# Summing the experts' outputs in DRAM with accumulating indirect transfers instead of one-hot matmuls, and a fourth weight slot while the experts run

## What is computed

```
aff = softmax(xt @ w_router)
gate, idx = top_k(aff.T, cap)                      # cap = 2 * n / 16
xe = take(xt, idx)
hid = silu(xe @ w_gate) * (xe @ w_up)
ye = (hid @ w_down) * gate[..., None]
y = zeros_like(xt).at[idx.reshape(-1)].add(ye.reshape(-1, D))
x = x + gt2 * y
```

## Time and profile before

| | |
|---|---|
| median of 3 runs | 3823.74 us (3815.38 to 3830.78) |
| the profiled execution's own time | 3816.27 us |
| its span | 3814.5 us |
| TensorE busy | 3627.5 us, 95% |
| VectorE busy | 1238.6 us, 32% |
| ScalarE busy | 832.8 us, 22% |
| GpSimd busy | 92.1 us, 2% |
| mean TensorE clock granted | 0.979 |
| moved by the DMA engines | 655.29 MB, mean 172 GB/s |

### The profile page before, as it was taken

How to read it: one execution, slowest core, us unless ns; L and a number is a source line. 1 busy time by engine, 2 the same in 40 slices (tenths; PEclk the granted TensorE clock), 3 DMA queues, 4 the chain that set the end, 5 groups by cost and what they waited for, 6 DMA issues and landing times.

```text
span 3814.5 us, 49841 instructions
## 1 busy us (share of the span) xinstructions
PE 3627.5 (95%) x21913; PEld 2043.0 (54%) x21913; DVE 1238.6 (32%) x2319; ACT 832.8 (22%) x1791; POOL 92.1 (2%) x112
## 2 busy tenths in 40 slices
PE   6999999998999799999999999999999988999997
PEld 3557777775555334343455577677655543443433
DVE  1444333337441400000142644333463531000102
ACT  2122112225332211100121311221343330110101
POOL 1000000000100000010000000000000000000000
PEclk9999999999999899999999999999999998999999
DMA  7332342323242599989742332341522327999892
GB/s 203 94 74 83 84 115 59 94 45 124 88 163 76 189 375 379 369 304 329 279 127 67 101 91 69 87 103 37 160 68 95 130 75 282 386 377 349 301 338 102
DMA packets 213272, 655.29 MB, mean 172 GB/s; under 512 B 8970, under 2 KB 21496, under 8 KB 209344
## 3 DMA queue, kind: packets, MB, share of 16 engines
q1 hardware_dynamic: 199680, 615.54, 47.5%
q0 software_dynamic: 7568, 23.32, 2.4%
q10 hardware_dynamic: 5808, 13.24, 0.9%
HBM read 600.45 MB, written 51.61 MB: 171 GB/s over the span
## 4 chain that ended last, share of the span: by engine, by line
PE 89%; DMA 5%; DVE 3%; ACT 2%; issue 1%; ACTq 0%; POOL 0%; DVEq 0%; SPq 0%; POOLq 0%
PE unit L735 11%; PE unit L683 10%; PE unit L1206 10%; PE work L1209 8%; PE work L1206 6%; PE unit L747 3%; PE unit L726 3%; PE work L1160 3%; PE unit L1105 3%; PE unit L766 3%; DMA ring<-in_w_e_gate 3%; PE unit L677 3%; PE unit L1054 2%; PE work L931 1%; PE work L936 1%; PE unit L693 1%
## 5 line engine op out<-in xcount | busy, mean ns | idle before, releaser
L735 PE MATMUL unit<-hT,ring 128*128 128x512 f32 x1024 | 478.5, 593 | 0.0
L1206 PE MATMUL unit<-ring,arena 128*64 128x512 f32 x2048 | 464.0, 600 | 2.6 <-ACT arena L1647 2.1
L1209 PE MATMUL work<-ring,arena 128*32 128x256 f32 x6144 | 367.2, 382 | 6.0 <-DMA ring<-in_w_e_gate 5.8
L1206 PEld LDWEIGHTS unit<-ring,arena 128*64 128x64 f32 x2048 | 141.1, 138 | 289.9 <-issue 283.9
L1209 PEld LDWEIGHTS work<-ring,arena 128*32 128x32 f32 x6144 | 182.0, 109 | 207.4 <-issue 93.2
L735 PEld LDWEIGHTS unit<-hT,ring 128*128 128x128 f32 x1024 | 176.5, 191 | 131.9 <-issue 131.9
L1206 PE MATMUL work<-ring,arena 128*64 128x512 f32 x1024 | 234.2, 599 | 4.0 <-ACT arena L1661 2.1
L683 PE MATMUL unit<-hT,ring 128*128 128x512 f32 x512 | 221.1, 592 | 0.0
L683 PE MATMUL unit<-arena,ring 128*128 128x512 f32 x384 | 166.8, 592 | 0.0
L683 PEld LDWEIGHTS unit<-hT,ring 128*128 128x128 f32 x512 | 96.7, 190 | 118.6 <-issue 118.6
L2101 DVE COPY arena<-work 64x512 f32<-64x512 f32 x32 | 22.2, 694 | 421.9 <-PE work L1206 421.9
(11 more groups left out here) (405 smaller groups left out, 4856.4 us busy)
## 6 DMA issues: line engine op xcount, KB each, us to landing
ring<-in_w_e_gate SPq DMA_DIRECT2D x64, 2048.0 KB, 11.5
ring<-in_w_e_up SPq DMA_DIRECT2D x64, 2048.0 KB, 9.6
ring<-in_w_e_down SPq DMA_DIRECT2D x64, 2048.0 KB, 10.7
ring<-in_w_in SPq DMA_DIRECT2D x32, 2048.0 KB, 15.0
ring<-in_w_ada SPq DMA_DIRECT2D x24, 2048.0 KB, 9.2
spill<-xT SPq DMA_DIRECT2D x110, 256.0 KB, 9.9
arena<-spill SPq DMA_DIRECT2D x20, 1280.0 KB, 7.3
ring<-in_w_out SPq DMA_DIRECT2D x4, 2048.0 KB, 7.9
```

The lines of the kernel that those rows point to most:

```text
L735: last = mm(bank[:, :], w[:, k, m * P:(m + 1) * P], hT[:, k, 0:TS], start=k == 0, stop=k == KD - 1)
L1206: last = mm(big[SLS * c:SLS * c + SLS, :], x, w[:, kk, 512 * c:512 * c + 512], start=k == 0, stop=k == KD - 1)
L1209: last = mm(low[SLOTP * c:SLOTP * c + SLOTP, 0:256], xp, w[:, kk, 256 * c:256 * c + 256], start=k == 0, stop=k == KD - 1)
```

## The change

The one-hot products are gone, and with them `ST`, `STP`, `iota`, the side work and the last pass. A tensor `moe_sum` of 640 rows in DRAM takes their place in each layer:

- During the attentions POOL clears it with five copies of 512 KB from a block of zeros in the constants, DRAM to DRAM.
- The copies of an expert's results multiply by the gate and write all 80 rows to one of three tiles `Y`.
- POOL adds these 80 rows to the rows of `moe_sum` with one indirect accumulating transfer, two experts behind the gathers in its order, each one only after the one before has landed.
- After the last of them ACT reads `moe_sum` back (five transfers of 512 KB into `ysum`), TensorE turns it, and DVE adds it to `xT` as before.

Beside this, the space of `h2tok` is a fourth slot for weights while the experts run (`slot_of`, `slot_before`): its first chunk waits for the stores of `h2_rows`, and chunk c then waits for chunk c - 4.

The diff, cut to its core:

```diff
-SIDE_SLOTS = [(_e, _w) for _e in range(1, NE + 1) for _w in "dm"]
-PASSES = [range(0, 4), range(4, 6), range(6, 8)]
...
+MRING = RING + 1
+assert PRE_CHUNKS % RING == 0 and NMOE % MRING == 0
+
+
+def slot_of(c):
+
+    l, q = c // LAYER_CHUNKS, c % LAYER_CHUNKS
+    if q < PRE_CHUNKS:
+        return q % RING, l * (PRE_CHUNKS // RING + NMOE // MRING) + q // RING + 1
+    s, n = (q - PRE_CHUNKS) % MRING, (q - PRE_CHUNKS) // MRING + 1
+    if s == RING:
+        return s, l * (NMOE // MRING) + n
+    return s, (l + 1) * (PRE_CHUNKS // RING) + l * (NMOE // MRING) + n
+
+
+def slot_before(c):
+
+    l, q = c // LAYER_CHUNKS, c % LAYER_CHUNKS
+    if q < RING:
+        return c - MRING
+    if q < PRE_CHUNKS + MRING:
+        return c - RING
+    return c - MRING
 
 
...
+        ring.append(at(15872, (4096,)))
...
-        YP = [at(13824, (D,))] + [at(8192 + D * g, (D,)) for g in range(NPT - 1)]
-        Ysc = [at(14848, (D,))] + [at(D * j, (D,)) for j in range(NPAIR - 1)]
-        ST = hT[:, 0:7, :].rearrange("p k t -> p (k t)")[:, 0:NPAIR * TS].rearrange("p (j t) -> p j t", j=NPAIR)
-        STP = hT[:, 7, 0:NPT * TP].rearrange("p (j t) -> p j t", j=NPT)
+        Y = [at(D * i, (D,)) for i in range(NROWS)]
+        ysum = at(15872, (NT, D))
...
-                    name, value = chunk_used(c - RING)
+                if c == PRE_CHUNKS + RING or c == LAYER_CHUNKS + PRE_CHUNKS + RING:
+                    sp.wait_ge(sig["rows_moved"], 16 * NT * (2 * (c // LAYER_CHUNKS) + 1))
+                elif c >= RING:
+                    name, value = chunk_used(slot_before(c))
                     sp.wait_ge(sig[name], value)
...
+                for t in range(NT):
+                    pool.dma_start(moesum[l][tile_t(t), :], A["consts"][:, CSTW:CSTW + D]).then_inc(sig["scattered"], 16)
...
-                for e in range(NE):
-                    if e >= NROWS:
-                        pool.wait_ge(sig["rows_turned"], l * NE + e - NROWS + 1)
-                    pool.indirect_dma_start(picked[e % NROWS][0:SL, :], None, h2rows[l],
-                                            bass.IndirectOffsetOnAxis(token[:, e:e + 1], 0))\
-                        .then_inc(sig[f"rows{e % NROWS}_loaded"], 16)
+                for e in range(NE + 2):
+                    if e < NE:
+                        if e >= NROWS:
+                            pool.wait_ge(sig["rows_turned"], l * NE + e - NROWS + 1)
+                        pool.indirect_dma_start(picked[e % NROWS][0:SL, :], None, h2rows[l],
+                                                bass.IndirectOffsetOnAxis(token[:, e:e + 1], 0))\
+                            .then_inc(sig[f"rows{e % NROWS}_loaded"], 16)
+                    if e >= 2:
+                        s = e - 2
+                        pool.wait_ge(sig["left_copied"], l * NE + s + 1)
+                        pool.wait_ge(sig["right_copied"], l * NE + s + 1)
+                        pool.wait_ge(sig["scattered"], 16 * (l * (NT + NE) + NT + s))
+                        pool.indirect_dma_start(moesum[l], bass.IndirectOffsetOnAxis(token[:, s:s + 1], 0),
+                                                Y[s % NROWS][0:SL, :], None, compute_op=ALU.add)\
+                            .then_inc(sig["scattered"], 16)
 
 
...
                         expert_chunk(e - 1, "d0")
-                        side_work((e, "d"))
                         expert_chunk(e - 1, "d1")
-                        side_work((e, "m"))
...
+                pe.wait_ge(sig["rows_moved"], 32 * NT * (l + 1))
                 for half in range(2):
                     for k in range(4):
-                        for g in range(NPT):
-                            last = mm(W[3 + half][:, tile_t(k)], YP[g][:, tile_t(4 * half + k)], STP[:, g, :],
-                                      start=g == 0, stop=g == NPT - 1)
-                    last.then_inc(sig["scatter_computed"], 1)
+                        last = tr(W[3 + half][:, tile_t(k)], ysum[:, NTS, tile_t(4 * half + k)], ident)
+                    last.then_inc(sig["sum_turned"], 1)
                 for k in range(KD):
                     if k >= 1:
                         pe.wait_ge(sig["x_added"], XADDS * (l + 1) - KD + k - 1)
-                    scatter(W[2 + 2 * (k % 2)], 2, k)
+                    for t in range(NTS):
+                        last = tr(W[2 + 2 * (k % 2)][:, tile_t(t)], ysum[:, t, tile_t(k)], ident)
+                    last.then_inc(sig["sum_turned"], 1)
...
+                    n = l * NE + e
+                    if e >= NROWS:
+                        act.wait_ge(sig["scattered"], 16 * (n - NROWS + 1 + NT * (l + 1)))
+                    y = Y[e % NROWS]
+                    a_(y[0:SLS, 0:512], W[2][0:SLS, :], ACT.Copy, scale=gsam[0:SLS, e:e + 1])
                     for c in range(2):
-                        last = a_(YP[e // 4][rp:rp + SLOTP, 256 * c:256 * c + 256],
-                                  W[5][SLOTP * c:SLOTP * c + SLOTP, 0:256], ACT.Copy)
+                        r = slice(SLOTP * c, SLOTP * c + SLOTP)
+                        last = a_(y[SLS:SLS + SLOTP, 256 * c:256 * c + 256], W[5][r, 0:256], ACT.Copy,
+                                  scale=gpro[r, e:e + 1])
                     last.then_inc(sig["left_copied"], 1)
 
                 keep_rows(0)
...
+                act.wait_ge(sig["scattered"], 16 * (NE + NT) * (l + 1))
+                for t in range(NT):
+                    act.dma_start(ysum[:, t, :], moesum[l][tile_t(t), :]).then_inc(sig["rows_moved"], 16)
...
-                for j in range(NPAIR):
-                    TSC(ST[:, j, :], iota[:, 0:TS], scol[:, 0, j:j + 1], scol[:, 1, j:j + 1], ALU.is_equal, ALU.mult)
-                for g in range(NPT):
-                    last = TSC(STP[:, g, :], iota[:, TS:T], pcol[:, 0, g:g + 1], pcol[:, 1, g:g + 1],
-                               ALU.is_equal, ALU.mult)
-                last.then_inc(sig["slots_ready"], 1)
+                v_.tensor_copy(gsam, W[2][:, 0:NE])
...
+                    TSC(y[0:SLS, 512:1024], W[2][SLS:2 * SLS, :], gsam[SLS:2 * SLS, e:e + 1], None, ALU.mult)
```

More of the change, by code:

```diff
@@ L102 @@
 FIRST_UNITS = KD + 2
-SIDE_SLOTS = [(_e, _w) for _e in range(1, NE + 1) for _w in "dm"]
-PASSES = [range(0, 4), range(4, 6), range(6, 8)]
-SIDE_WORK = [("scatter", _p, _k) for _p in range(2) for _k in range(KD)]
-SIDE, _at = {}, 0
-for _w in SIDE_WORK:
-    _at = max(_at, SIDE_SLOTS.index((2 * PASSES[_w[1]][-1] + 3, "d")))
-    SIDE[SIDE_SLOTS[_at] if _at < len(SIDE_SLOTS) else "rest", _w] = _at
-    _at += 1
-SIDE = [_s for _s in SIDE]
-SIDE_NO = {_w: _i for _i, (_s, _w) in enumerate(SIDE)}
-NROWS = 3
-XADDS = 10 + len(PASSES) * KD + 2
-def side_at(slot):
-    return [w for s, w in SIDE if s == slot]
-def side_before(e):
-    return sum(1 for s, w in SIDE if s != "rest" and s[0] < e)
-assert PRE_CHUNKS % RING == 0 and NMOE % RING == 0
+NROWS = 3
+XADDS = 12 + KD
+MRING = RING + 1
[15 more added lines that the diff above has]
+    return c - MRING
 def moe_no(l, e, part):
@@ L190, in constants @@
     put("sin", np.sin(ang) * sign)
-    put("iota", np.broadcast_to(np.arange(T), (P, T)))
     put("eps", np.full((P, 1), EPS))
@@ L315, in build @@
         ring = sb("ring", RING * 4096)[:, :].rearrange("p (s w) -> p s w", s=RING)
+        ring = [ring[:, s, :] for s in range(RING)]
         cst = sb("cst", CSTW)
@@ L411, in build @@
         h2rows = [nc.dram_tensor(f"h2_rows{l}", [T, D], F32).ap() for l in range(DEPTH)]
+        moesum = [nc.dram_tensor(f"moe_sum{l}", [T, D], F32).ap() for l in range(DEPTH)]
         xspill = nc.dram_tensor("x_spill", [DEPTH, P, KD * T], F32).ap()
@@ L661, in chunk_in @@
             def chunk_in(c):
[L662 to L663 removed]
+                s, n = slot_of(c)
+                pe.wait_ge(sig[f"chunk{s}_loaded"], 16 * n)
+                return ring[s].rearrange("p (k n) -> p k n", n=512)
             def used(ins):
@@ L1626, in _ @@
                 act.wait_ge(sig["logits_rowed"], l + 1)
-                act.dma_start(iota, A["consts"][:, CSTW:CSTW + T]).then_inc(sig["iota_loaded"], 16)
                 a_(affT[0:NE, 0:TS], W[2][0:NE, :], ACT.Copy)
```

94 lines of the change are left out of this document (27 added, 67 removed).

## The result

The kernel after takes 3727.45 us (median of 4 runs, 3722.23 to 3731.65), the kernel before beside it 3819.56 us (4 runs, 3813.97 to 3830.78). The ratio is 0.9758, 95% interval [0.9738, 0.9779]. The side (faster) was right; the forecast 3779 was 52 us too high. All executions count in the medians of this document but one, of 9418.13 us, in the version six_slots, whose other five lie between 3722.37 and 3727.05 us.

A forecast was written before the change was run, and what follows sets the result against it. TensorE and the DMA engines were both taken as full in the experts, the transfers binding after the change. 3816.3 - 60.7 (experts) + 16.5 (tails) = 3772 us, plus 7.5 to the median: 3779, range 3742 to 3850.

The forecast's parts named there:

- the step from the profiled execution to the median: Whole kernel: the median of the runs shown lies 7.5 us above the profiled execution, so 3772 becomes 3779.
- The transfers' pace, 36.0 us an expert: In the experts: the transfers allow 33.4 + 2.6 = 36.0 us an expert, above TensorE's 33.77.
- The base, 33.4: In the experts: weights and a gather take 33.4 us an expert, the middle of 33.0 and the measured 33.84.
- The accumulation, 2.6 us: In each expert: an accumulating transfer costs a gather, 1.8 us, and one more read of 0.33 MB, 0.8.
- The fourth slot: In the weights' ring: lets one more chunk be in before the first is used up; a deeper ring helps no further.
- The formula with 92 chunks: In a layer's experts: 5.6 + 92 x 36.0/6 + 5.6 = 563.2 us, 60.7 less over both layers.
- Removed side work, 44.2 us a layer: In the experts: pieces of four products cost 30.0 us, of two 14.2; the gain if TensorE alone set the pace.
- The tails, +16.5: After each layer's experts: (16.7 - 6.3 + 3) + (6.4 - 6.3 + 3) = 16.5 us lost, bounds 0 and 35.
- The cold clock: In the tails: TensorE waits over 15 us and then runs at the lower clock level, 3 us a layer.
- What is hidden: Beside other work: POOL's clears (13 us, covered by 83), its later gathers and the next layer's vectors cause no waits.
- Cheap accumulation: Rival, in the experts: an accumulation below 1.8 us leaves TensorE setting the pace, 3752 us; chance 0.20.
- the share of 1.0 throughout: Sign in the experts after: a DMA share of 1.0 throughout; below 0.95 with a pace above 35 would be wrong.

The follow-up runs named there:

- six_slots: The kernel after with a ring of six weight slots instead of four while the experts run; 3724.43 us, ratio 0.9767.
- before_4slots: The kernel before with the fourth weight slot alone, one-hot products and side work kept; 3802.19 us, ratio 0.997.
- no_acc: The kernel after, with four slots, without the accumulating transfers, so the sum read back lacks the experts' results; 3699.47 us, ratio 0.9701.

## Why the prediction was right and wrong

The side, faster, was right, but in part by luck. By the prediction's own sum the change without the fourth slot would have taken one chunk's use, 6 us, more in each layer, some 3791 us; it took 3811.83, no less than before. The mechanism was wrong where it matters, in the experts.

By its steps (52 us too high: 34.6 in the experts, 7.1 in the tails, 2.7 elsewhere, 7.8 in the step from the profiled execution to the median):

- **The transfers' pace, 36.0 us an expert,** is the step that failed, and with it the reading behind it, "a deeper ring helps no further, since the engines have no idle time to fill". With a deep ring the pace is 34.1 to 34.3. By the prediction's own formula the transfers decide the time only from about 35.2 us on. Below that its forecast would have been that of TensorE, 551.3 and 547.4 us for the experts, and that is 27.7 of the 34.6. The pace had two terms, and either of them, had it been right, would have brought it down to about that limit:
  - The base, 33.4, should have been about 32.3 (an estimate, from 34.1 less an accumulation). I had pulled it up towards 33.84, the pace measured in the kernel before, since I read the share of 1.02 as full engines. The same share goes with 360 to 392 GB/s in the table above, and before_4slots shows that 33.84 was TensorE's 33.71 and the ring's waits, and no reading of the transfers. The earlier trace rows alone gave 33.0.
  - The accumulation, 2.6 us, took about 1.8 with a deep ring. With the ring of three it took 2.3, tails included, and the pace was 34.9 without accumulations and 37.1 with.
- **The fourth slot.** I gave it one chunk's lead, 6 us a layer. With the accumulations it is worth 3811.83 - 3727.45 = 84 us, without them 3737.92 - 3699.47 = 38, in the kernel before some 12. The two parts of the change don't add up: neither the new way of adding up results nor the slot gives more than 0.3% without the other.
- **The formula with 92 chunks** isn't what made the forecast high. For 34.1 us it gives 534 us, less than TensorE's 543.2, so no wait at all, and the experts took 546.0 and 545.9. For the 35.9 of two accumulations it gives 561.7, and with four slots they took 566.2. It misses some 3 to 5 us of waits a layer.
- **Removed side work, 44.2 us a layer.** Right in mechanism and in size: with four slots and no waits in either, the experts take 587.6 us with the side work (before_4slots) and 543.2 and 543.6 without it (no_acc), a difference of 44.4 and 44.0. The gain measured is larger (49.6 and 45.7), because the waits that three slots had cost the kernel before (7.9 and 4.0) went too, and only 2.8 and 2.3 came back.
- **The tails, +16.5.** Measured 6.6 and 2.8, where the steps gave 13.4 and 3.1. In layer 0 I took 9.4 us for the last accumulation's landing, since weights still arrive; from its issue to the read-back's were 5.3. The read-back took 13.0 as predicted (13.4), so 22.5 us stand where I had 26.7; layer 1 took 18.2 against 16.4. The steps after that and the cold clock together gave 5.9 and 5.4 back, where I had 3.3. The cold clock is in the windows after the read-back (columns as above; the clock is the third number from the end): TensorE had been almost idle for 20 us, and was granted 0.50, the lower of the levels of 1.2 and 2.4 GHz, then 0.77, then full speed. Lost of full speed are up to 5 x 0.50 + 6 x 0.23 = 3.9 us, where I had 3.

```profile
1855.00:1860.00 5.00, 3.94 (x16) 3.14 (x16) 3.08 (x10) 0.74 (x1) 0.00 (x0) 0.50 0.01 2
1860.00:1866.00 6.00, 5.99 (x29) 2.62 (x30) 1.24 (x2) 1.48 (x3) 0.00 (x0) 0.77 0.09 8
1866.00:1880.00 14.00, 13.72 (x88) 7.50 (x86) 3.75 (x5) 4.96 (x10) 0.00 (x0) 1.00 1.02 254
```

- **What is hidden** was right: clears (the first layer's experts start at 1288.43 against 1289.28, and the stretch up to the second layer's took 1224.4 against 1226.2), gathers (landing at most 10.7 us; TensorE waits for two of 32, the first of each layer), vectors (in 13.1 us after the last copies, before the read-back).
- **The rivals.** "Cheap accumulation" came nearest, with 3752 and a chance of 0.20; the price measured with a deep ring, 1.6 to 1.8 us, is at or just under its limit of 1.8. It missed by 25: 7.8 from the median's offset, 7.1 from the tails, 2.7 elsewhere, and 6.9 mostly from the waits of the kernel before. Of the signs that the prediction named, the share of 1.0 throughout came, and the pace near 36.0 did not: 33.71 is the cheap case's.
- **The Trainium skill's rules.** By "DMA: Bandwidth & Descriptors" (Anatomy of one DMA) I had estimated 0.75 us for the bytes of an accumulation; the engines' time was 1.5 to 1.8, and 0.7 for a plain write of the same rows. This one core moved more than its figure of about 358 GB/s for a core from its HBM (Specifications): 392 GB/s over 250 us. The same page gives 358 as what each of two cores gets when both draw on the same HBM (Bandwidth); the kernel runs on one, and no run here has a second at work. By 358 the result would have been slower than before.

## What to carry to other kernels

In these runs a DMA share of 1.0 meant that a transfer was always outstanding, not that the rate was at its limit: with the same transfers it went with 360 GB/s in three slots and 392 in four. Compare the GB/s of several stretches, and set the landing time of a load against the time that the ring allows it, (slots - 1) times the use of one chunk. If the landing times grow along a loop, the transfers are the slower side, and depth buys only lead; if they are flat and TensorE still waits for single chunks, try one slot more before saving bytes: here it gave 84 us, where leaving out all accumulations gave 74. Before costing a burst (a gather, an accumulation) at its engine time, ask whether two of them can fall on the same chunk. And work that leaves a loop lands in its tail: here the read-back's wait for the last accumulation makes 18 us of the 25 by which all accumulations lengthen the span.

## What the runs showed of the hardware

- An indirect accumulating transfer of 80 rows of 4 KB takes POOL 1.42 us to issue (a gather 0.93). It lands after 5.1 us at least, where a gather of the same rows has 3.9, and after 8.4 in the median, where the gather has 9.0. Lines L662 and L654 of the kernel after, with their landing times:

```profile
L662 POOL DMA_INDIRECT moe_sum<-arena,slotu x32: 1392/1421/1487, 1337.7 to 3666.0; - x32
...
DMA to landing us min/median/max: 5.1/8.4/9.3
```

```profile
L654 POOL DMA_INDIRECT arena<-h_rows,slotu x32: 896/926/1009, 1281.7 to 3573.8; - x32
...
DMA to landing us min/median/max: 3.9/9.0/10.7
```

- It takes 1.5 us of all sixteen engines (1.8 with four slots). A plain write of the same rows takes 0.7, so about half is the read and add.
- Loads issued ahead of a gather held it up: with two more chunks of 2048 KB outstanding it was there 8.0 us after its issue instead of 4.2, and holding the two back undid that.
- Not settled: why a chunk that an accumulation and a gather both hit falls back by more than their engines' time. The change without the fourth slot loses about 3 us an expert against TensorE's pace, and about 1 even without accumulations. Whether the load of single engines is uneven there wasn't measured, nor what the gather's place in the loop does.
